# The prompt runs alone through output projection and first MLP while the samples still read pages; the samples follow in strips on weights read a second time and join at the gate half

## The reference, cut to what matters

```python
for l in range(2):
    h = rms_norm(y, rms_mix_g[l])              # prompt and samples
    if l == 0:                                 # retention || differential attention
        rq, rk, rv, rg, dq, dk, dv = split(h @ w_in)
        ro = head_group_norm(retention(rope(rq), rope(rk), rv, s0)) * silu(rg)
        q, k = rope(rms_norm(dq, qg)), rope(rms_norm(dk, kg))
        # samples: k, v = concat(cache[page_table], new row)
        a = softmax(q1 k1) - lam * softmax(q2 k2)
        do = rms_norm(a @ v, sub_g) * (1 - lam_init)
        mix = concat(ro, do) @ w_out           # 1536 -> 1024
    else:                                      # gMLP
        u, v = split(gelu(h @ w_in), 2)        # 1024 -> 2 x 3072
        v = layer_norm(v, ln_g, ln_b)          # a sample's v row is an output
        mix = (u * (tril(w_s) v + b_s)) @ w_out
    y = y + mix
    y = y + square(relu(rms_norm(y, g) @ w_up)) @ w_down    # 1024 -> 4096 -> 1024
```

## Time and profile before

| what | value |
|---|---|
| device time, median of 3 | 2015.98 us (2014.85 to 2016.22) |
| the profiled execution | 2021.46 us, its span 2019.8 us |
| first part, to the first matmul of `oe` | 0 to 704.1 us |
| `oe` and first MLP | 704.1 to 1141 us |
| `v`, layer norm and gate blocks | 1141 to 1360 us |
| from `u0` on | 1360 to 2019.8 us |
| TensorE's mean granted clock | 0.927 |

### The profile page before, as it was taken

The page is one execution under the profiler, slowest core; times in us unless marked ns, Lnnn a source line. Parts: engine busy times, 40 slices in busy tenths (PEclk is TensorE's granted clock), DMA queues, the critical chain, the costliest instruction groups (busy, mean ns, idle before and its releaser), DMA issues.

```text
span 2019.8 us, 35464 instructions
## 1 busy us (share of the span) xinstructions
PE 1812.8 (90%) x14049; PEld 1643.4 (81%) x14049; DVE 1010.6 (50%) x1311; ACT 583.3 (29%) x928; POOL 436.0 (22%) x522
## 2 busy tenths in 40 slices
PE   6767878677787699999999999989999999999998
PEld 5654545455564399999999999979999999999997
DVE  2899867888994535332343343253323344323321
ACT  5322222323233223221232223253224332212311
POOL 2222211233333002320340100024204223102400
PEclk9887776887888699999999999989999999999999
DMA  4558655699997722332323222212322323233231
GB/s 125 187 168 288 228 195 186 210 342 350 340 364 235 244 86 82 104 115 86 93 84 105 76 64 80 65 39 81 105 84 84 105 84 94 94 94 93 85 97 61
DMA packets 202094, 288.03 MB, mean 143 GB/s; under 512 B 13041, under 2 KB 149954, under 8 KB 201682
## 3 DMA queue, kind: packets, MB, share of 16 engines
q1 hardware_dynamic: 178432, 214.75, 32.7%
q0 software_dynamic: 21168, 68.64, 10.1%
q10 hardware_dynamic: 2362, 2.83, 0.4%
HBM read 274.96 MB, written 11.21 MB: 142 GB/s over the span
## 4 chain that ended last, share of the span: by engine, by line
PE 77%; DVE 8%; issue 6%; DMA 5%; ACT 3%; POOLq 1%; POOL 0%; SPq 0%; ACTq 0%; DVEq 0%
PE ps L1795 18%; PE ps L1797 18%; PE ps L1796 18%; PE ps L1591 5%; PE ps L1593 4%; PE ps L1592 4%; DMA vbuf<-in_cache_v 3%; PE ps L1626 2%; DVE kbuf L1247 2%; DVE Sc L1250 2%; PE ps L1695 1%; PE ps L1869 1%; POOLq L530 1%; PE ps L1534 1%; DMA xst<-in_x_prompt 1%
## 5 line engine op out<-in xcount | busy, mean ns | idle before, releaser
L520 DVE TENSOR_TENSOR w_lo<-raw,w_hi 128x1024 fp32r<-128x1024 f32 x238 | 327.7, 1384 | 456.5 <-ACT w_hi L513 455.3
L1795 PE MATMUL ps<-xg_hi,w_hi 128*128 128x260 f32 x1408 | 397.9, 283 | 1.0 <-DVE vn L1509 1.0
L1797 PE MATMUL ps<-xg_hi,w_lo 128*128 128x260 f32 x1408 | 397.8, 283 | 0.0
L1796 PE MATMUL ps<-xg_lo,w_hi 128*128 128x260 f32 x1408 | 396.6, 282 | 0.0
L513 ACT ACTIVATE w_hi<-raw 128x1024 fp32r<-128x1024 f32 x248 | 259.1, 1054 | 432.5 <-PE ps L1797 399.5
L1591 PE MATMUL ps<-w_hi,xg_hi 128*128 128x256 f32 (+1 forms) x1056 | 321.5, 304 | 6.9 <-DVE xg_lo L1423 4.1
L1592 PE MATMUL ps<-w_lo,xg_hi 128*128 128x256 f32 (+1 forms) x1056 | 311.7, 295 | 0.0
L1593 PE MATMUL ps<-w_hi,xg_lo 128*128 128x256 f32 (+1 forms) x1056 | 311.0, 294 | 0.0
L1797 PE MATMUL ps<-h_hi,w_lo 128*128 128x260 f32 x1024 | 289.3, 283 | 0.0
L1795 PE MATMUL ps<-h_hi,w_hi 128*128 128x260 f32 x1024 | 289.1, 282 | 0.0
L1796 PE MATMUL ps<-h_lo,w_hi 128*128 128x260 f32 x1024 | 288.3, 282 | 0.0
(11 more groups left out here) (283 smaller groups left out, 2535.0 us busy)
## 6 DMA issues: line engine op xcount, KB each, us to landing
kbuf<-in_cache_k SPq DMA_DIRECT2D x256, 256.0 KB, 4.5
vbuf<-in_cache_v POOLq DMA_DIRECT2D x256, 256.0 KB, 4.6
raw<-in_w_ffn_up SPq DMA_DIRECT2D x64, 512.0 KB, 3.8
raw<-in_w_ffn_down SPq DMA_DIRECT2D x64, 512.0 KB, 3.4
raw<-in_w_in_odd SPq DMA_DIRECT2D x48, 512.0 KB, 3.6
raw<-in_w_in_even SPq DMA_DIRECT2D x36, 512.0 KB, 6.2
raw<-in_w_out_odd SPq DMA_DIRECT2D x24, 512.0 KB, 3.5
raw<-in_w_out_even SPq DMA_DIRECT2D x12, 512.0 KB, 3.4
```

The source lines that it names most:

```text
L520: dve.tensor_tensor(w_lo[:, c.slot], raw[:, c.slot % 2], w_hi[:, c.slot].bitcast(F32), ALU.subtract).then_inc(lo_made, 1)
L1795: pe.matmul(out, wh, xh, start=kk == 0, stop=False, skip_group_check=True)
L1796: pe.matmul(out, wh, xl, start=False, stop=False, skip_group_check=True)
L1797: mm_ = pe.matmul(out, wl, xh, start=False, stop=kk == KC * groups - 1, skip_group_check=True)
```

## The change

`plan()` puts one page step in each slot of m = 2 to 17: 80 of the 150 (with `K` 0 to 79 and `V` 0 to 29). The other 70 stand after the chunks of `oe` and of the MLP, 8 in 5 chunks, until `dn00`. From `up01` on the samples go through `oe`, up, down and `v` by themselves: 50 quads `W` of those weights, 1 MB each, are read again by POOL into the slots of `vbuf`, 5 in 4 chunks, and PE multiplies each with the samples as stationary operand in four strips, as a `V` does; `pvO` and `pvT` fold each of 18 blocks of 512 columns. The wide phases and `v` take 512 tokens. For the first three, `wide` has one matmul of 512 columns in place of two of 260. Loops of these phases are written out. The samples' layer norm stands in `v`, and at `u0` both groups are together again. The samples' rope in m = 0 to 4 has steps of its own (`sq1`, `sq2`).

```diff
+L0 = ("oe", "up00", "dn00", "up01", "dn01")
+DENSE = [(n, mac, g) for n in L0 + ("v",) for mac in range(PHASES[n][2]) for g in range(PHASES[n][1])]
+W_BLOCKS = [("oe", c, 3) for c in range(2)] + [("up", c, 2) for c in range(8)] + [("dn", c, 8) for c in range(2)] + [
+    ("vv", c, 2) for c in range(6)]
...
         for t in range(NT + 1):
-            for n in range(2):
-                if step < STEPS and (m, t) >= (2, NT) and (n == 0 or m not in (3, 4)):
-                    after[m, t] += kv_step(step)
-                    step += 1
-                if n == 0:
-                    after[m, t] += middle[m, t]
+            after[m, t] += kv_step(step) + middle[m, t]
+            step += 1
             after[m, t] += late[m, t]
...
+    while step < STEPS:
+        for _ in range(2 - i % 5 % 2):
+            if step < STEPS:
+                put(i, *kv_step(step))
+                step += 1
+        i += 1
+    put(i, ("fa",))
+    put(i + 1, ("fb",))
+    fifths = 5 * (i + 3)
+    for n, (b, g) in enumerate(W_QUADS):
+        phase, c, groups = W_BLOCKS[b]
+        at = fifths // 5
+        fifths += 4
+        put(at, ("W", n))
+        if g == groups - 1:
+            put(at, ("pvO", NS + b))
+            put(at + 1, ("pvT", NS + b))
...
+            def quad_in(u):
+                if u < NQ + NW:
+                    wait(pool, v_used, u - Q_SLOTS + 1)
...
+                    else:
+                        b, g = W_QUADS[u - NQ]
+                        phase, c, _ = W_BLOCKS[b]
+                        rows = S_OF[phase][0].rearrange("(g k p) n -> g p k n", k=QUAD, p=P)[g]
+                        pool.dma_start(dst[:, :, :], rows[:, :, 512 * c:512 * c + 512]).then_inc(done, 16)
...
+                    elif kind == "V" and i > 0:
+                        quad_in(i - 1 + Q_SLOTS)
+                    elif kind == "W":
+                        quad_in(NQ + i - 1 + Q_SLOTS)
...
+                        if name in L0:
+                            for g in range(2):
+                                pool_steps((name, 2 * i + mm, g))
                         for b in range(2):
                             make(b, 4 * i + 2 * mm + b)
...
+                elif kind == "W":
+                    pe.wait_ge(v_loaded[u % Q_SLOTS], quad_landed(u))
+                    for j in range(QUAD):
+                        at = P // QUAD * j
+                        last = pe.matmul(ps[at:at + NS, PV[b % 2], :], S_OF[phase][1][:, QUAD * g + j, :], vbuf(u)[:, j, :],
+                                         start=g == 0, stop=g == groups - 1, skip_group_check=True)
...
-                            for blk in range(2):
+                            for blk in range(2 if name in L0 else 0):
+                                for k in range(KC):
+                                    kk, cols = KC * g + k, slice(P * blk, P * blk + P)
+                                    wh, wl = w_hi[:, c.slot, k, cols], w_lo[:, c.slot, k, cols]
+                                    xh, xl, out = src_hi[:, kk, 0:SEQ], src_lo[:, kk, 0:SEQ], acc_p(s, blk)
+                                    pe.matmul(out, wh, xh, start=kk == 0, stop=False, skip_group_check=True)
+                                    pe.matmul(out, wh, xl, start=False, stop=False, skip_group_check=True)
+                                    mm_ = pe.matmul(out, wl, xh, start=False, stop=kk == KC * groups - 1, skip_group_check=True)
...
-                    for t in range(NT + 1):
+                    for t in range(NT):
+                        pe.wait_ge(nat_read, NT * (N_IN + mac) + t - 1)
+                        natural(cs, t, NAT[t % 2], NT - 1)
```

More of the change, by code:

```diff
@@ L170, in plan @@
     tail = after[N_IN, NT]
[L171 to L177, removed]
     while s <= NS or b < 12:
@@ L185, in plan, with put @@
                 b += 1
-    tail += [("fb",), ("so",)]
+    tail.append(("so",))
+    for key in DENSE + ["end"]:
+        after[key] = []
+    def put(i, *steps):
+        after[DENSE[i] if i < len(DENSE) else "end"].extend(steps)
+    i = 0
+    while step < STEPS:
[15 more added lines that the diff above has]
+            put(at + 1, ("pvT", NS + b))
+            if (phase, c) in (("oe", 1), ("dn", 1)):
+                e = 1 if phase == "oe" else 2
+                put(at + 1, ("sr", e))
+                put(at + 2, ("ss", e))
+                fifths = 5 * (at + 3)
+    put(at + 2, ("l1",))
+    put(at + 3, ("l2",))
+    for i in range(6):
+        put(at + 4 + i // 2, ("l3", i))
     return after
 AFTER = plan()
-ORDER = [s for m in range(N_IN + 1) for t in range(NT + 1) for s in AFTER[m, t]]
+FIRST = [s for m in range(N_IN + 1) for t in range(NT + 1) for s in AFTER[m, t]]
+ORDER = FIRST + [s for key in DENSE + ["end"] for s in AFTER[key]]
+K1 = sum(s[0] == "K" for s in FIRST)
+NV1 = sum(s[0] == "V" for s in FIRST)
 TURN_FILL = {s: i for i, s in enumerate([s for s in ORDER if s[0] in ("turn", "dT")])}
 OUT_FILL = {s: i for i, s in enumerate([s for s in ORDER if s[0] in ("qb", "snew", "dB", "rB", "pvT")])}
+OUT_FIRST = sum(s[0] in ("qb", "snew", "dB", "rB", "pvT") for s in FIRST)
 def constants():
@@ L343, in build @@
         Qb = r("Qb", [P, 2, 512])
+        ptb = r("ptb", [1, NS * NPAGES], I32)
+        tiny = r("tiny", [P, 528])
+        sqs = r("sqs", [NS, 512])
+        mTs = r("mTs", [P, 12, NS])
+        xgs = r("xgs", [P, KD, NS])[:, :, :]
+        hs = r("hs", [P, 32, NS])
+        misc = r("misc", [P, 96])
+        s_at = r.at
+        h_at = s_at + 4 * 4096
+        r = Region(base, kv_at)
+        doN = r("doN", [P, NT, 512])
+        r = Region(s_at, h_at)
+        dvn = r("dvn", [P, NT, 512])
+        smp_at = r.at
+        smp = r("smp", [NS, 3, 512])
+        sks, svs, srq = (smp[:, i, :] for i in range(3))
+        srk = sks
+        srg4 = r("srg4", [P, DVR])
+        part = r("part", [P, CW])
+        r = Region(s_at, smp_at)
+        v3 = r("v3", [P, 1024], F32R)
+        k3 = r("k3", [P, 512], F32R)
+        o4 = r("o4", [P, DVR])
+        scm = r("scm", [P, P])
+        r = Region(smp_at, h_at)
+        kmask = r("kmask", [P, 2, 512], F32R)
+        qTm = r("qTm", [P, H, NS * NS])
+        r = Region(h_at)
         rqT = r("rqT", [P, H, SEQ])
@@ L700, in step, with between, square @@
                             pool.wait_ge(mid_hi_made, n + (MID0[name] + 1))
-                            pool.tensor_tensor(one(ll, n), tmp2[:, b, :], one(hh, n).bitcast(F32),
+                            pool.tensor_tensor(one(ll, n), tmp2[:, b, 0:w], one(hh, n).bitcast(F32),
                                                ALU.subtract).then_inc(mid_lo_made, 1)
-                repeat(pool, PHASES[name][2] // 2, step, first=1)
-            def square(name):
+                n = PHASES[name][2] // 2
+                repeat(pool, n, step, first=n if name in L0 else 1)
+            def between(name, e=None):
+                for mac in range(PHASES[name][2]):
+                    for g in range(PHASES[name][1]):
+                        pool_steps((name, mac, g))
+                    if e is not None:
+                        for b in range(2):
+                            add_square(e, 2 * mac + b)
+            def square(name, w=T):
                 def make(b, n):
@@ L761, in _ @@
                 add_square(3, n)
-            mlp(1)
+            for h in range(2):
+                mids(f"up1{h}", square(f"up1{h}"), h_hi, h_lo)
         @block.scalar
@@ L1843, in v_step @@
                             squares(2)
[L1844 to L1850 removed]
+                        if mac == 1 and t == 2:
```

730 lines of the change are left out of this document (459 added, 271 removed).

## The result

The changed kernel takes 2055.4 us (median of 4, 2051.2 to 2060.5) against 2016.1 us: a ratio of 1.0197 (95% interval 1.0173 to 1.0221). I had forecast 1983 us, within 1945 to 2024. It is slower, and outside the range.

What follows compares the result with a forecast made beforehand. Bound by waiting in the first 704 us, by PE's work in the last 1316. Terms -136 - 30 - 34 - 3 + 92 + 25 + 7 + 46 = -33 us: profiled 2021.5 to 1988.5, at the median 1983; range 1945 to 2024.

Steps and rivals of the forecast that it cites:

- the first part: Up to the first 512-column matmul: fewer key pairs and value quads shorten 704 us to 568, -136 us.
- well under 0.9: Sign for m = 11 to 17: the transfers' share there, with the stretch taking 168 us.
- quads: Wide part: 34 `V` and 50 `W` quads cost PE 1.1 us each, +92 us.
- New waits, +46: Wide part: PE waits in `up00` (+18), `oe` (+4), `up01` (+12), starts, `v` and tables (+12); ends +20 and +75.
- the rest: Other wide-part work: quads +92, folds +25, small pieces +7, `v` -34, gate stage -3, and what stays unchanged.
- would be 2 us a macro: `up00`: POOL's pages land at 14 us where PE wants 12; counted within DVE's +18, not added.
- two `W` in one key: `up01`: the second quad lands at 11 us, wanted at 6.4; two places, 5 us and slow clock each, +12.
- three signs that I had named: Forecast wrong if PE's quad waits pass 80 us, the interval is 235 ns, or m = 8 and 9 take 120 us.
- the clock after a wait: Wide part: 2 us for the slow start, and slow clock behind two waits in `up01`, inside its +12.
- the interval: `oe` and MLP: a 512-column matmul every 222 ns (213 to 235), -30 us, ends -46 and -6.
- Quads wait in POOL's queue everywhere: Rival: PE waits at each `V` and `W`, 1.7 us a quad, 141 us for 46: 2078 us; chance 0.17.
- DVE blocked by POOL: Rival: in `up00` each of 26 key multiplies is held 0.64 us, +17 us: 2000 us; chance 0.08.

Runs made afterwards that it cites:

- e2: Changed kernel with POOL's reduction of the maximum over partitions replaced by a plain copy for samples 5 to 7: 2040.3 us, 1.0114.
- e7: Changed kernel with the gate stage's five loads issued by SP in `up01` instead of POOL at the head of `dn01`: 2038.2 us, 1.0136.
- e5: Changed kernel with each 512-row weight quad loaded as four transfers of 128 rows, still issued by POOL: 2052.2 us, 1.018.
- e9: Changed kernel with POOL issuing quad n + 2, not n + 1, at its step of quad n from `oe` on: 2028.2 us, 1.0085.
- e11: Changed kernel with earlier quad issue, gate loads on SP, softmax shift by PE matmul (samples 5 to 7), weight quads 0.9 chunk apart: 1982.7 us, 0.9863.
- e1: Changed kernel with the samples' 50 weight quads issued by SP instead of POOL, at the same keys: 2087.1 us, 1.0361.

## Why the prediction was wrong

**Right: the first part.** -136 forecast, -134 measured. Its pieces were less good: +8, -22, -14, -19, -83 and -4 us, where I had -3, -17, -22, -18, -66 and -10. `m` = 2 to 5 took 102.6 us for 94.8. I had counted on 20 key pairs for 22; but DVE was behind its plan before, and in the trace 18 pairs stand in this stretch now where 16 stood, 5 of the 7 us that DVE is busier. `m` = 11 to 17 took 150.9 for the 168 forecast, beyond my end of -80, at clock 0.97 for 0.86: once the pages are halved PE hardly waits, transfers still at 0.89, where I had said "well under 0.9". The errors cancelled: that the sum is right to 2 us is luck.

**Right: quads.** Undisturbed, the gap that a quad makes between two wide matmuls is 1.30 us (median of 33), of which 0.23 is the matmul's own: 1.07 for my 1.1.

**Wrong: "New waits, +46".** This is the step that failed. The wide part was to take 759 us and took 819.8. The 61 us are these:

| term of the wide part | forecast | measured |
| --- | --- | --- |
| 1824 wide matmuls at full clock | 405 (222 ns each) | 420 (230.5 ns) |
| the same, slow clock | 2 | 21 |
| new waits of PE | 46 | 74 |
| the rest | 306 | 305 |

The waits are those over 0.5 us, 86 us in all, less the 12.8 us that the same list has before (704 to 1360 us). Two things made them. First, I counted what POOL computes (squares, 5.4 us) and its page issues (0.97), but not what it does outside its busy time. The reduction's row in the list of groups is small, so I gave it nothing: 17 us by e2. The gate stage's five loads stand in POOL's order at the head of `dn01`, and I costed none: 12 by e7. I had no term either for the 5 us and more that POOL stands behind each 1 MB issue, but by e5 that one costs nothing. Second, the place: POOL issues a quad one step after its slot is free. I saw it for two `W` in one key (12 us), not for all (23 by e9). These three come to 52 us by the ratios, against 28 us more of waits and 19 more of slow clock behind them than forecast. I wrote in `up00` that POOL's lateness "would be 2 us a macro" behind DVE; in fact DVE was busy two thirds of the 149 us, and the waits were POOL's. None of the three signs that I had named came true (71 us of waits at quads for 80, 230 ns for 235, 108.6 us at `m` = 8 and 9 for 120): each term stayed short of its own limit, and their sum didn't.

**Wrong: the clock after a wait.** Waits bring the lower clock behind them: `up00` has 0.88 and `dn01` 0.92, where `dn00`, which hardly waits, has 0.99, as the MLP had before. Around the wait of 13.5 us that ends at 759.7:

```profile
746.20:759.70 13.50, 0.00 (x0) 0.00 (x0) 8.98 (x8) 4.95 (x7) 8.44 (x11) 0.69 0.49 168
759.70:764.20 4.50, 4.48 (x14) 2.28 (x15) 2.66 (x4) 0.88 (x2) 2.85 (x4) 0.50 1.05 402
```

The clock falls during the wait, and the first 4.5 us of work behind it are granted 0.50 (1.2 GHz): some 2 us more for that wait. Over the wide matmuls 21 us went so, for the 2 of the forecast. e11, with fewer waits, pays 13 by the same count. I had added a slow clock only in `up01`.

**Wrong by size: the interval.** 230 ns, near the upper end of my range (213 to 235), 15 us. It lies between a fixed cost (224) and a tenth (235): 256 columns more cost 112 ns, where 2.4 GHz would make 107. I had taken the 1 ns between 256 and 260 columns as a sign of the first, which it couldn't be: the two differ by 0.1 ns over 4 columns. The Trainium skill ("TensorE: Matmul & The Clock Gate", Wait — 56ns, not 53.3ns?) has 2.5 ns over the columns, 215.7 ns here; the runs measured 230, so for this kernel's matmuls the trace decides against it.

**The rivals.** "Quads wait in POOL's queue everywhere" is what happened in place and cause, except that in `dn00` (no wait) and `v` (0.5 us) they hardly do; its price was smaller (71 us over 84 quads is 0.84 a quad, below the 0.94 from which I let it decide) and the sign still turned, since clock and interval took 34 us more. "DVE blocked by POOL" wasn't tested by a run of its own, but the trace of `up00` speaks against it:

```profile
L1422 DVE TENSOR_TENSOR kbuf<-kbuf,Qb 128x1024 f32<-128x1024 f32 x26 | 31.6, 1216 | 3.5 <-DMA kbuf<-in_cache_k 3.5
```

All 26 key multiplies took 1.21 to 1.23 us, and none ran while POOL computed. Only `w_lo` was stretched as before, 7 times of 15 (1.95 us for 1.21), some 5 us on an engine that wasn't the bound.

That e11 lands at 1982.7 us, on the forecast, doesn't make the forecast right: it has 13 us of slow clock (2 forecast) and 15 of interval in it that I hadn't counted, and 26 us of new waits, counted as above, where I had allowed 46.

## What to carry to other kernels

An engine that issues transfers for another must be costed by everything in its order: look at its idle gaps without a releaser as well as its busy time, and find by a run which of them are waited for (those at a reduction cost 17 us here, those behind the 1 MB issues nothing), and ask of each issue whether it stands where its slot becomes free or a step behind it; moving it one step brought 23 us here, moving it to an emptier queue that waits for something else (e1) cost 33. Where work moves out of a stage with slack into one that PE fills, a wait is paid as itself and again, in part, as slow clock behind it (21 us beside 86 here). And when a change is slower but half of it is right (134 us gained in the first part), look for the removable waits of the other half before giving it up: three edits of a few lines took it from 1.0197 to 0.9929, a fourth to 0.9863.

## What the runs showed that I had not expected

- A reduction over partitions on POOL: 0.39 us busy, 10.3 us idle before and 7.0 behind it, without a releaser (739.56). With a copy in its place the 7.0 are gone and 7.8 in front remain, as a wait for DVE. Three of them cost 17 us of kernel time.
- A 1 MB transfer of 512 rows, issued by POOL: where nothing else holds POOL, the next issue mostly follows 5.7 to 6.5 us later, and it lands 5.6 to 6.1 us after its own (medians by tensor). As four of 128 rows: 2.1 us of issues, and the kernel's time stays.
- Five small loads (weights of the gate stage, two of them of single elements) hold POOL 17.7 us; issued by SP, the kernel is 12 us faster.
- Wide matmuls in fp32r at full clock: 230 ns for 512 columns, beside 118 for 256.
- After 13.5 us without work PE was granted half its clock for the next 4.5 us of work.
